# A depthwise convolution's sample part, per head as windowed products and sums instead of tap by tap

## What is computed

```python
a = cv * jax.nn.sigmoid(cg)
full = jnp.concatenate([buf.astype(a.dtype), a], axis=1)
y = lax.conv_general_dilated(full, w[:, None, :].astype(a.dtype), window_strides=(1,),
                             padding='VALID', dimension_numbers=('NWC', 'WIO', 'NWC'),
                             feature_group_count=a.shape[-1])
c = y + b                      # then layernorm, silu, and the product with w_co
```

## Time and profile before

| | |
|---|---|
| median of 3 runs | 941.18 us (940.92 to 941.48) |
| span of the profiled execution | 940.7 us |
| TensorE matmul busy | 928.3 us (99%) |
| VectorE busy | 772.2 us (82%) |
| ScalarE, GpSimd busy | 464.4 us (49%), 106.7 us (11%) |
| convolution taps on the prompt, L1917 | 120, 97.6 us |
| granted TensorE clock, mean | 0.996 of full speed |

### The profile page before, as it was taken

The page is one execution under the profiler, slowest core; times in us unless marked ns, Lnnn a source line. Parts: engine busy times, 40 slices in busy tenths (PEclk is TensorE's granted clock), DMA queues, the critical chain, the costliest instruction groups (busy, mean ns, idle before and its releaser), DMA issues. The chain is left out here.

```text
span 940.7 us, 18449 instructions
## 1 busy us (share of the span) xinstructions
PE 928.3 (99%) x6833; PEld 907.8 (96%) x6833; DVE 772.2 (82%) x1231; ACT 464.4 (49%) x684; POOL 106.7 (11%) x110
## 2 busy tenths in 40 slices
PE   8999999999999999999999999999999999999996
PEld 8999999999999999999999999999999999999995
DVE  6899985988698869876455569999888999889997
ACT  6654452445336324634833345456545555455664
POOL 3011330042006001500231000000000000000001
PEclk9999999999999999999999999999999999999998
DMA  6245216211620352042342222233222223232122
GB/s 219 68 150 198 69 57 224 90 45 56 246 90 23 134 191 90 23 150 87 117 140 68 89 73 84 90 108 106 102 90 91 90 68 113 90 116 109 46 91 100
DMA packets 22460, 98.56 MB, mean 105 GB/s; under 512 B 2929, under 2 KB 5122, under 8 KB 17909
## 3 DMA queue, kind: packets, MB, share of 16 engines
q1 hardware_dynamic: 19576, 77.13, 24.9%
q0 software_dynamic: 1984, 19.72, 5.7%
q10 hardware_dynamic: 832, 0.88, 0.3%
HBM read 85.28 MB, written 12.44 MB: 104 GB/s over the span
## 5 line engine op out<-in xcount | busy, mean ns | idle before, releaser
L1301 PE MATMUL ps<-h_hi,w_hi 128*128 128x288 f32 x896 | 193.7, 298 | 0.0
L1301 PE MATMUL ps<-h_lo,w_hi 128*128 128x288 f32 x896 | 191.7, 295 | 0.0
L1301 PE MATMUL ps<-h_hi,w_lo 128*128 128x288 f32 x896 | 191.4, 295 | 0.0
L793 ACT ACTIVATE w_hi<-raw 128x1024 fp32r<-128x1024 f32 x76 | 80.4, 1058 | 177.4 <-PE ps L1301 174.2
L1301 PEld LDWEIGHTS ps<-h_hi,w_hi 128*128 128x128 f32 x896 | 143.5, 189 | 1.3 <-issue 0.6
L1301 PEld LDWEIGHTS ps<-h_hi,w_lo 128*128 128x128 f32 x896 | 144.3, 189 | 0.0
L1301 PEld LDWEIGHTS ps<-h_lo,w_hi 128*128 128x128 f32 x896 | 144.2, 188 | 0.0
L1692 DVE TENSOR_TENSOR w_lo<-raw,w_hi 128x1024 fp32r<-128x1024 f32 x76 | 94.2, 1240 | 48.9 <-ACT w_hi L793 48.8
L1917 DVE SCALAR_TENSOR_TENSOR conv<-a_p,vec,conv x120 | 97.6, 813 | 0.2
L1569 PE MATMUL ps<-cols_b,late 128*128 128x288 f32 x432 | 62.8, 295 | 0.1
L1569 PE MATMUL ps<-cols_a,main 128*128 128x288 f32 x432 | 62.9, 295 | 0.0
(11 more groups left out here) (362 smaller groups left out, 1857.3 us busy)
## 6 DMA issues: line engine op xcount, KB each, us to landing
raw<-w_head_in SPq DMA_DIRECT2D x40, 512.0 KB, 3.5
raw<-w_fp_in SPq DMA_DIRECT2D x18, 1024.0 KB, 4.9
cs<-st_c_in POOLq DMA_DIRECT2D x4, 2048.0 KB, 9.6
c_s_out<-cs POOLq DMA_DIRECT2D x4, 2048.0 KB, 7.7
raw<-w_fo_in SPq DMA_DIRECT2D x8, 1024.0 KB, 4.9
x<-xT_in SPq DMA_DIRECT2D x16, 288.0 KB, 4.1
raw<-w_cgcv_in SPq DMA_DIRECT2D x8, 512.0 KB, 3.6
raw<-w_ga_in SPq DMA_DIRECT2D x8, 512.0 KB, 3.5
```

Of the source, the lines that this page charges most:

```text
L793: act.activation(w_hi[:, s, :], raw[:, s, :], ACT.Copy).then_inc(hi_ready, 1)
L1301: last = pe.matmul(ps[:, 2 * s + b, 0:HALF], wt[:, w, k * P:k * P + P], src[:, k, b * HALF:b * HALF + HALF], start=(k == 0 and wt is w_hi ...
```

## The change

In each round of the head loop, `conv_tap` keeps the prompt's part alone, and waits with `steps.settle()` for all steps before it. The samples' part moves to two calls of `sample_conv`, each for four of the eight sequences: one `tensor_tensor` product of overlapping windows of `a_s` with all 31 taps (4 sequences x 8 tokens x 31 taps = 992 products a partition, into `tmp`), and one `reduce_sum` along the taps into the 32 output columns; the second call is followed by `sample_bias`, which adds the bias to all 64. The two calls stand behind `lo_of(0)` and `lo_of(1)`. The count of VectorE's steps in a round goes from 89 to 63. Nothing else differs.

```diff
-DVE_HEAD_STEPS = 89
+DVE_HEAD_STEPS = 63
@@
                 def conv_tap(w):
 
-                    out = row(conv, h)
+                    o, a = row(conv, h)[:, 0:TP], row(a_p, h)[:, w:w + TP]
                     wcol = vcol(h * CW + (V_WDW + w))
-                    outs = (out[:, 0:TP], out[:, TP:T].rearrange("p (b j) -> p b j", b=SB))
-                    ins = (row(a_p, h)[:, w:w + TP],
-                           a_s[:, bass.ds(h, 1), :, w:w + SL].rearrange("p o b n -> p (o b) n"))
-                    for o, a in zip(outs, ins):
-                        if w == 0:
-                            steps.on(dve.tensor_scalar(o, a, wcol, vcol(h + V_BDW), ALU.mult, ALU.add))
-                        else:
-                            steps.settle(back=1)
-                            steps.on(dve.scalar_tensor_tensor(o, a, wcol, o, ALU.mult, ALU.add))
+                    if w == 0:
+                        steps.on(dve.tensor_scalar(o, a, wcol, vcol(h + V_BDW), ALU.mult, ALU.add))
+                    else:
+                        steps.settle()
+                        steps.on(dve.scalar_tensor_tensor(o, a, wcol, o, ALU.mult, ALU.add))
+
+                def sample_conv(half):
+
+                    n = SB // 2
+                    rows_ = a_s[:, bass.ds(h, 1), half * n:half * n + n, 0:SL]
+                    dims = [list(d) for d in rows_.ap]
+                    windows = bass.AP(rows_.tensor, rows_.offset, [dims[0], dims[2], dims[3], [dims[3][0], CW]])
+                    taps_ = vec[:, bass.ds(h * CW + V_WDW, CW)].unsqueeze(1).unsqueeze(1).broadcast_to([P, n, SL, CW])
+                    terms = tmp[:, :, :].rearrange("p a n -> p (a n)")[:, 0:n * SL * CW]
+                    steps.on(dve.tensor_tensor(terms.rearrange("p (b j w) -> p b j w", b=n, j=SL), windows, taps_, ALU.mult))
+                    at = TP + half * n * SL
+                    steps.settle()
+                    steps.on(dve.reduce_sum(row(conv, h)[:, at:at + n * SL], terms.rearrange("p (m w) -> p m w", w=CW),
+                                            axis=mybir.AxisListType.X))
+                    steps.settle()
+
+                def sample_bias():
+                    o = row(conv, h)[:, TP:T]
+                    steps.on(dve.tensor_scalar(o, o, vcol(h + V_BDW), None, ALU.add))
@@
                 lo_of(0)
+                sample_conv(0)
                 lo_of(1)
+                sample_conv(1)
+                sample_bias()
```

## The result

The changed kernel takes 947.27 us (median of 4 runs, 946.65 to 948.09), the kernel before 941.33 (940.92 to 941.66, 4 runs beside them): ratio 1.0058, 95% interval 1.0044 to 1.0072. It is slower, by 5.9 us (0.6%); forecast were 946.4 and a loss of 5.2. The profiled span went from 940.7 to 946.5.

A forecast was written before the change was run, and what follows sets the result against it. TensorE, busy 354.0 of 354.0 us through the head loop, was taken as the bound. Stalls of 3.31 us in round 0 and 1.89 in the others, 5.2 on the 941.18 median, gave 946.4 us; range 941.5 to 953.5.

The forecast's parts named there:

- The tap period: VectorE's prompt taps (L1917) still start 0.94 us apart with the sample taps gone; bounds 0.88 and 0.67.
- rival 2: Not slower: a dependent tap costs no more than an independent one, period 0.67 us; 941.6 us, chance 0.20 with neighbours.
- Product and sum: On VectorE, each 992-column product and each sum along taps takes 1.18 us.
- rival 3: A sum along taps costs 2.82 us on VectorE, each adding 1.64; 18.3 us lost, 959.5 us, chance 0.08.
- Split of unit 4 in round 0: VectorE's split for unit 4 in round 0 starts at 92.70 us instead of 87.56.
- Unit 4's wait in round 0: TensorE waits 2.34 us for unit 4's split, ready at 94.07 us where unit 4 wanted 91.73.
- S3 in round 0: TensorE's score product S3 waits for S0's late multiplication on VectorE: a stall of 0.97 us.
- The gap at the loop's jump: VectorE's 5.10 us of issue idle ahead of the mask row goes with a shorter loop, about 2 to 1.
- Rival 1: The gap at the loop's jump stays, unit 4 is late every round; 11.1 us lost, 952.2 us, chance 0.25.
- Rounds 1 to 3: Unit 4's split is in time by 0.34 us; S3 stalls 0.63 each round, 1.89 in all.
- The sum: Round 0's 3.31 us plus 1.89 for the other rounds make a loss of 5.2 us.
- The clock: TensorE's waits of 1 to 3 us shouldn't lower its clock; 3.4 us idle in the first 40 left 1.00.

The follow-up runs named there:

- static_taps2: Changed kernel with prompt taps at fixed addresses: every round convolves block 0, the prompt part of the other blocks left out; 944.36 us, ratio 1.0027.
- before_plus: Kernel before, all its taps kept, with the change's products, sums and bias made in addition into a spare tile; 971.19 us, ratio 1.0322.
- pad72b: Changed kernel with 72 increments of an unused semaphore on VectorE in each round, 335 instructions a round; 961.64 us, ratio 1.0209.
- end: Changed kernel with both sample_conv calls and the bias moved behind unit 8's gate product, hf as scratch; 942.99 us, ratio 1.0012.
- two_places: Changed kernel with the first sample call ahead of the first product at L1991, the second with the bias behind unit 8's gate product; 946.43 us, ratio 1.0051.
- start_pool: Changed kernel with sample_conv(0) ahead of lo_of(0) and GpSimd's first subtraction of a round held until unit 7's split is done; 943.93 us, ratio 1.0029.
- pad40b: Changed kernel with 40 increments of an unused semaphore on VectorE in each round, 303 instructions a round; 947.32 us, ratio 1.0059.
- after_again: The changed kernel run once more, unchanged; 947.27 us against 941.13, ratio 1.0063.
- pool_wait2: Changed kernel with only GpSimd's first subtraction of a round (L729) held until unit 7's split is done; 947.02 us, ratio 1.0058.

## Why the prediction was right

- **The tap period (0.94).** Right: 0.93 to 0.94, and rival 2 fell. The reason, wait and then address arithmetic, is shown by static_taps2, and that the samples' taps ran for next to nothing beside it by before_plus (0.18 us for 9 of them). Even with fixed addresses a dependent tap isn't free (0.79 against 0.67), which was rival 2's premise.
- **Product and sum (1.18 each).** Right: 1.18 and 1.19 in all eight calls. The sum along taps costs what the product costs, and rival 3 fell. The row behind rival 3, 2.91 us for the 1024 columns of L1983, was no price of such an instruction: it stands at 126.82, beside a GpSimd product from 125.51 to 128.65. In pad72b, where GpSimd had finished before, the same subtraction (L2004 at 132.84) took 1.22.
- **Split of unit 4 in round 0 (92.70).** It started at 92.30; the first split came 0.23 earlier than in the trace of before, which leaves 0.17.
- **Unit 4's wait in round 0 (2.34).** Mis-sized by little: the wait is 2.40, and from unit 3 to unit 4 it is 9.05 instead of 6.40, so 2.65. TensorE came sooner, since its first three units of the loop took 18.80 instead of 19.18 us, at the same granted clock of 1.00. I know of no cause, but executions differ so without the change: between 66 and 84 us end ran 141 matmuls and two_places 137, and these two kernels are the same up to there (the kernel before ran 138, the changed one 141). With unit 4 itself (6.36 instead of 6.40) the net is 2.65 - 0.38 - 0.04 = 2.2.
- **S3 in round 0 (0.97).** This is the term that failed: the S part grew by 15.96 - 14.02 = 1.94. VectorE was as late as worked out. What was left out is that GpSimd's subtraction sets in there. It started at 107.08 before, 0.03 before the end of unit 7's split, and that split was already over when it could have been hurt. In the changed kernel GpSimd starts at 109.07 and the split at 109.27. start_pool gives the size, 1.08 us, which with 0.97 makes 2.05. The step that let it through: the split of unit 7 was moved to a new place at its old price, and GpSimd was looked for only at the products' place (the last sentence of the prediction), where it has no arithmetic to do between 72.2 and 107.08 us. Rows 3 end at 107.02. A few lines further the trace of before does show it:

```profile
109.77 1.59 DVE L1917 SCALAR_TENSOR_TENSOR conv<-a_p,vec,conv  x1
...
113.16 1.33 DVE L1917 SCALAR_TENSOR_TENSOR conv<-a_s,vec,conv  x1
114.42 1.79 DVE L1917 SCALAR_TENSOR_TENSOR conv<-a_p,vec,conv  x1
```

- **The gap at the loop's jump (goes).** Right, at the 2 to 1 given. pad40b and pad72b show that the loop's length decides. Rival 1 is what pad72b shows.
- **Rounds 1 to 3 (unit 4 in time by 0.34, S3 0.63 each).** Right in kind: the margin is 0.55, which includes the 0.15 I had counted off, so 0.40. The S part grew by 0.38 a round instead of 0.63; what makes the difference wasn't looked into. There the split (199.25) starts ahead of GpSimd (199.52) and isn't long.
- **The sum.** Loop: 2.2 + 1.94 + 3 x 0.38 = 5.3 measured, 5.2 forecast. The near agreement is partly luck: the term missing in round 0 (1.0) is made up by rounds 1 to 3, cheaper by 0.75, and by unit 4's wait, cheaper by 0.1 net. The 0.7 behind the loop was not forecast; it is no more than executions scatter by.
- **The clock.** The forecast that waits of this size don't lower it was wrong in one of the two profiled executions of the changed kernel. It cost no time, since the slower unit 4 let VectorE catch up ahead of S3. The forecast's ground was also misread: the 3.4 us of idle in the first 40 us are no single wait but three (2.19, 0.66 and 0.54 us), the longest of them ahead of the first matmul.

## What to carry to other kernels

A chain of dependent short steps that alternates with another chain has the second one for nearly nothing: before taking such a filler away, look at the starts of the main chain, not at the filler's busy time. Work that an engine has room for over a round may still be late at one place; move it by where its followers are due, and look then for what the other engines start at that place. When an instruction is forecast to move, read the trace of every engine past the place where it lands.

## What the hardware did that I had not expected

**VectorE and GpSimd.** A VectorE instruction whose two inputs lie in SBUF and that begins while GpSimd subtracts took 2.30 us instead of 1.22 (split), up to 1.83 instead of 0.75 (tap) and up to 1.33 instead of 0.28 (samples' tap). A cast with one input in SBUF grew as well: `kv_hi` took 1.39 us at 117.37 in the kernel before, and 0.28 in before_plus at 212.74, where GpSimd stood still. Where the split began first it kept its 1.22 and GpSimd's subtraction was longer instead. Three subtractions took 3.75 us before (107.08). They took 4.86 in round 0 of the changed kernel, where the second one had to wait for the split, and 4.99 in round 1, where the split began ahead of the first:

```profile
107.08 3.75 POOL L729 TENSOR_TENSOR cs_lo<-cs,cs_hi 128x512 fp32r<-128x512 f32 x3 [30.19 <-ACT cs_hi L933]
```
```profile
109.07 4.86 POOL L729 TENSOR_TENSOR cs_lo<-cs,cs_hi 128x512 fp32r<-128x512 f32 x3 [32.41 <-ACT cs_hi L933]
...
199.52 4.99 POOL L729 TENSOR_TENSOR cs_lo<-cs,cs_hi 128x512 fp32r<-128x512 f32 x3 [39.76 <-ACT cs_hi L933]
```

In these cases whoever is second waits for the other's instruction to end, by an estimate from these rows: 109.07 + 3.75 / 3 = 110.32, and 110.32 + 1.22 - 109.27 = 2.27, measured 2.30. The score products, which read one input from PSUM, didn't grow beside it: two took 1.36 at 107.02, with GpSimd from 107.08, and one product of as many columns with both inputs in SBUF takes 0.68 alone (L1945 above). The Trainium skill (SBUF — State Buffer, Who interferes with whom) says that two SBUF inputs on VectorE contend with a GpSimd instruction that reads SBUF, that the shared port pair is an exclusive lock, and that issue order decides who blocks. These rows agree. One case doesn't fit by its recorded starts: in two_places GpSimd's subtraction at 118.41 takes 2.95 us, and the product that begins at 119.06, behind it, keeps its 1.18. Why GpSimd gave way there stays open. The Trainium skill (SBUF — State Buffer, Who interferes with whom) also says that a `tensor_reduce` never contends on trn2, and the trace agrees: in two_places it took 1.19 at 120.36, with GpSimd busy until 121.36. I had not weighed that section in the forecast.

**The clock.** After a wait of TensorE of 2.4 us for unit 4 the granted clock stayed at 1.00 (2.4 GHz) in two profiled executions (the changed kernel, pad40b) and fell to 0.5 (1.2 GHz) for some 3.4 us in others (after_again, pool_wait2, and with waits of 2.55 and 2.47 pad72b and before_plus), which made unit 4 longer by 1.5 us. The length of the wait alone doesn't decide: in before_plus it stayed up behind 1.76 us in round 1 and fell behind 1.74 us in round 3 (mean 0.81 from 378 to 384 us). What does decide wasn't settled.

**Loads of instructions.** A loop of 343 or 335 recorded VectorE instructions stood 5 to 6 us at each jump back, one of 303 or 263 didn't, and the loads fell from 33 or 34 to 18 or 19. The Trainium skill (Runtime: NRT & Kernel Launch, Instruction fetch mechanics) says that a taken branch stalls for a load where its target isn't in the window held. These runs agree; that the limit lies between 303 and 335 instructions, as the trace counts them, is shown by them alone.
